# Gate and up with x's high and low parts side by side, and matmuls on few rows padded to 128

## Chip, cores and metric
The kernel runs on one core of a Trainium2 chip. The metric is the device time of one execution in microseconds; of several runs the median counts.

## The reference
Two layers over x of 256 tokens and 1024 features, float32. Each layer is

```
x = LN(alpha*x + 0.5 * (silu(x@Wg) * (x@Wu)) @ Wd)      # feed-forward, D_FF = 2816
x = LN(alpha*x + mixer(x))                              # MLA attention | mLSTM | retention, gated
x = LN(alpha*x + 0.5 * (silu(x@Wg) * (x@Wu)) @ Wd)      # second feed-forward
```

The mixer projects x to latents, queries, keys, values and gates. The attention branch has 4 heads: `score = q_nope . k_nope (128 features) + q_rope . k_rope (64 rotated features)`, causal, with a softmax; k_rope is shared by the heads. The mLSTM branch has 4 heads with exponential gates, for which a row of values per head must be spread over all 128 partitions. All weights are float32 and are read once.

## The kernel before
**Arithmetic.** TensorE (PE) takes the large products as float32r. Each float32 weight and each x is split into a high part (what the cast to float32r keeps) and a low part (the rest), and a product is three matmuls: high x high, high x low, low x high. This is `tile3` (lines 1177 to 1181), once per 128 input rows, accumulated in PSUM over the 8 chunks of 128 features. Small products (scores, values, sums over partitions) use plain float32, which PE does in two passes; the trace shows such a matmul as x2.

**Weights.** SyncE loads them in units of 128 x 2048 elements (1 MB) into a ring of three slots `raw` (`load`, line 337). ScalarE (ACT) casts a unit to `whi` (`hi`, line 456), VectorE (DVE) writes the rest to `wlo` (`lo`, line 724), PE uses both. `hi` waits until PE has left the slot (`w_used`), the next load until `lo` has read it (`w_lo`).

**Feed-forward.** A step handles 256 of the 2816 hidden features: unit gate, unit up, unit down, 11 steps a network, in a hardware loop except for the first and last pieces. In gate and up (`two_chunks`, `features`) the stationary operand is a 128x128 tile of weights, the moving one 256 tokens of x; 2 column tiles x 8 chunks x 3 matmuls = 48 matmuls of 256 columns. Gate goes to PSUM bank 4, up to bank 5, both column tiles side by side in one bank. ACT takes silu of bank 4 (line 467), DVE multiplies it with bank 5 (line 737) into `hid`, then splits `hid` (lines 744, 746). Down (`tokens`, line 1235) is 24 matmuls of 512 columns, with `hid` stationary and the weights moving, into banks 0 to 3, where alpha*x was put first as transposes (`seed`, line 1199). The order on PE is gate of step f+1, up of f+1, down of f. So `hid` of a step is needed one gate and one up unit after its own, but in the last step only one down unit after up's end. Each engine's order is written out by hand: on DVE in a turn the gate weights' `lo`, the product, the up weights' `lo`, the split of `hid`, the down weights' `lo`; on ACT the `hi` of gate, silu, `hi` of up, `hi` of down. In the last step the product and the split of `hid` come before the `lo` of the last down unit.

**Layer norm.** After each sub-layer the rows are normalised and transposed back; x is split pair by pair of chunks (`split_x`, lines 767 and 769) and the first unit of the next sub-layer takes each pair as it comes.

**Mixer.** Its order is also written by hand. Projection units of 48 matmuls alternate with small pieces. `mla_scores(h)` (lines 1319, 1320) adds for each of two query blocks a matmul over 128 features and one over the 64 rotary features; q_rope holds two heads on top of each other, heads of even number on partitions 0 to 63, odd on 64 to 127. k_rope holds the same 64 rows twice. The heads' scores run in pairs (0,1) and (2,3). `spread(h)` (line 1371) multiplies a selecting matrix on 4 rows with `row_m` on 4 rows, 512 columns, to give head h's row on all partitions. It is called in two pairs too. `rotate` (lines 851 to 854) makes q_rope and the others on DVE.

Of the kernel before, what the change touches and what calls it, by code (L numbers as in the profile page):

```python
# [100 lines left out]
def build(nc, a):  # L101
# [17 lines left out]
    def sem(name):  # L119
        return ctx.enter_context(nc.semaphore(name))  # L120
# [10 lines left out]
    xhi, xlo = sb("xhi", [P, KC, SEQ], F32R), sb("xlo", [P, KC, SEQ], F32R)  # L131
# [23 lines left out]
    hlo_last = place("hlo_last", [P, 2 * SEQ], F32R, r_u2 + 10240)  # L155
    g_row = place("g_row", [P, D_MODEL], F32, r_u2 + 16384)
# [15 lines left out]
    row_m = place("row_m", [HEADS, 2 * SEQ], F32, r_rows + 3072)  # L172
# [10 lines left out]

    k_rope = place("k_rope", [P, SEQ], F32, r_b)
    q_nope = place("q_nope", [P, HEADS, SEQ], F32, r_b + 1024)
    q_rope = place("q_rope", [P, 2, SEQ], F32, r_b + 5120)
# [43 lines left out]
    par_ready = sem("par_ready")  # L230

    silu_done, prod_done, hid_hi, hid_lo = sem("silu_done"), sem("prod_done"), sem("hid_hi"), sem("hid_lo")
    rows_loaded = sem("rows_loaded")
# [179 lines left out]
    def _(pool):  # L413

        pool.wait_ge(w_loaded[RING - 1], 16)
# [34 lines left out]
    def _(act):  # L450
# [7 lines left out]
        def ffn(l, w):  # L458
# [4 lines left out]
            def silu_of(j, k, f):  # L463

                act.wait_ge(w_used, done_no(l, k, f))
                act.wait_ge(prod_done, step_no(l, w, j))
                act.activation(silu[:, :], ps[:, 4, :], ACT.Silu).then_inc(silu_done, 1)  # L467

            hi(l, base + 2)
            silu_of(0, base, 0)  # L470
            hi(l, base + 3)
            hi(l, base + 4)
            with act.Fori(0, NF - 2) as f:
                hi(l, base + 5, f)
                silu_of(f + 1, base + 2, f)
                hi(l, base + 6, f)
                hi(l, base + 7, f)
            silu_of(NF - 1, base + 2, NF - 2)
# [240 lines left out]
    def _(dve):  # L719
# [7 lines left out]
        def ffn(l, w):  # L727
# [4 lines left out]
            def product(j, k, f):  # L732

                dve.wait_ge(silu_done, step_no(l, w, j))
                dve.wait_ge(w_used, done_no(l, k, f))
                dve.wait_ge(hid_lo, step_no(l, w, j))
                dve.scalar_tensor_tensor(out=hid[:, :], in0=ps[:, 5, :], scalar=0.5 / ALPHA, in1=silu[:, :],  # L737
                                         op0=ALU.mult, op1=ALU.mult).then_inc(prod_done, 1)

# [10 lines left out]
            product(0, base + 1, 0)  # L750
# [3 lines left out]
            with dve.Fori(0, NF - 2) as f:  # L754
                lo(l, base + 5, f)
                product(f + 1, base + 3, f)
# [912 lines left out]
```

## Time and profile before

| | |
|---|---|
| median of 3 runs | 1429.93 us (1428.03 to 1430.86) |
| profiled execution | 1428.79 us, its span 1426.6 us |
| mean granted clock of PE | 0.988 |
| busy: PE / DVE / ACT / POOL | 1378.0 / 865.7 / 617.4 / 66.1 us |
| matmuls | 9848 |
| DMA | 234.22 MB, mean 164 GB/s |

The span runs from the first to the last instruction; the time of an execution is a little longer. Matmuls are pipelined: the length that a row gives for one is from its start to its modelled end, and the next starts before that end. What one costs PE is the distance from its start to the next one's. "PEld" is the load of the stationary operand, which overlaps matmuls. A form such as `64*128 64x256` is a stationary operand of 64 rows by 128 columns and a moving one of 64 rows by 256 columns. "x24" on a row merges that many instructions in sequence. A bracket at the end of a row is the idle time before it and what ended it.

### The profile page before, as it was taken

How to read it: one execution, taken by the hardware profiler on the slowest of the kernel's cores; microseconds unless marked ns; L12 is line 12 of the kernel's file. 1: busy time of each engine (PE TensorE's matmuls, PEld its weight loads, DVE VectorE, ACT ScalarE, POOL GpSimd, SP SyncE). 2: the span in 40 equal slices, each digit the busy share in tenths (PEclk: the TensorE clock that was granted, in tenths of full speed). 3: DMA queues.
4: the chain of work that ended last, by engine and by line, in shares of the span. 5: the costliest groups of instructions: out<-in, count | busy, mean ns of one | idle time of the engine just before them, and what ended most of it. 6: DMA issues, size and time to landing. Idle time of an engine off the chain costs nothing.

```text
span 1426.6 us, 23193 instructions
## 1 busy us (share of the span) xinstructions
PE 1378.0 (97%) x9848; PEld 1285.4 (90%) x9848; DVE 865.7 (61%) x884; ACT 617.4 (43%) x586; POOL 66.1 (5%) x58
## 2 busy tenths in 40 slices
PE   7999989999999999999999999899999999999997
PEld 7999979889899979999899999797988999899996
DVE  4554466688885655544555544675888756554555
ACT  4333344564354353333443333554744543533331
POOL 2960000000000000000000000000000000000000
PEclk9999999999999999999999999999999999999999
DMA  8655644533345446555445555445334555465551
GB/s 285 209 176 178 192 146 129 178 116 122 118 158 190 167 137 206 177 179 192 159 154 193 183 176 187 131 142 158 119 91 146 178 178 177 121 203 176 183 196 63
DMA packets 182313, 234.22 MB, mean 164 GB/s; under 512 B 5808, under 2 KB 161072, under 8 KB 182128
## 3 DMA queue, kind: packets, MB, share of 16 engines
q1 hardware_dynamic: 182016, 231.68, 50.7%
q0 software_dynamic: 240, 1.71, 0.4%
q8 instruction: 44, 0.72, 0.2%
q14 instruction: 13, 0.11, 0.0%
HBM read 232.33 MB, written 1.05 MB: 164 GB/s over the span
## 4 chain that ended last, share of the span: by engine, by line
PE 95%; DVE 3%; ACT 2%; DMA 0%; issue 0%; SPq 0%; DVEq 0%; ACTq 0%
PE ps L1179 23%; PE ps L1180 23%; PE ps L1181 23%; PE ps L1235 20%; PE ps L1199 1%; DVE wlo L724 1%; PE ps L1334 1%; PE ps L1320 1%; DVE z L828 1%; PE ps L1371 1%; PE ps L1319 1%; ACT whi L456 1%; PE ps L1352 0%; PE ps L1381 0%; PE ps L1376 0%; DMA z<-x 0%
## 5 line engine op out<-in xcount | busy, mean ns | idle before, releaser
L456 ACT ACTIVATE whi<-raw 128x2048 fp32r<-128x2048 f32 (+2 forms) x221 | 416.2, 1883 | 665.2 <-PE ps L1181 489.3
L724 DVE TENSOR_TENSOR wlo<-raw,whi 128x2048 fp32r<-128x2048 f32 (+2 forms) x221 | 497.5, 2252 | 310.7 <-ACT whi L456 310.6
L1179 PE MATMUL ps<-xhi,whi 128*128 128x256 f32 (+1 forms) x2304 | 660.2, 287 | 15.6 <-DVE xlo L769 10.4
L1180 PE MATMUL ps<-xlo,whi 128*128 128x256 f32 (+1 forms) x2304 | 655.4, 284 | 0.0
L1181 PE MATMUL ps<-xhi,wlo 128*128 128x256 f32 (+1 forms) x2304 | 655.0, 284 | 0.0
L1179 PEld LDWEIGHTS ps<-xhi,whi 128*128 128x128 f32 (+1 forms) x2304 | 441.5, 192 | 22.7 <-issue 14.1
L1180 PEld LDWEIGHTS ps<-xlo,whi 128*128 128x128 f32 (+1 forms) x2304 | 441.4, 192 | 3.0 <-issue 0.5
L1181 PEld LDWEIGHTS ps<-xhi,wlo 128*128 128x128 f32 (+1 forms) x2304 | 441.6, 192 | 1.0
L1235 PE MATMUL ps<-wlo,hhi 128*128 128x512 f32 x320 | 127.7, 399 | 0.0
L1235 PE MATMUL ps<-whi,hhi 128*128 128x512 f32 x320 | 126.1, 394 | 0.0
L1235 PE MATMUL ps<-whi,hlo 128*128 128x512 f32 x320 | 125.4, 392 | 0.0
L737 DVE SCALAR_TENSOR_TENSOR hid<-ps,silu 128x512 f32<-128x512 f32 x44 | 30.5, 692 | 117.7 <-PE ps L1181 91.2
L1235 PEld LDWEIGHTS ps<-whi,hlo 128*128 128x128 f32 x320 | 60.1, 188 | 14.4
L1235 PEld LDWEIGHTS ps<-whi,hhi 128*128 128x128 f32 x320 | 60.2, 188 | 13.7
L1235 PEld LDWEIGHTS ps<-wlo,hhi 128*128 128x128 f32 x320 | 60.1, 188 | 12.1
L1179 PE MATMUL ps<-yhi,whi 128*128 128x256 f32 x192 | 54.6, 284 | 0.0
L1181 PE MATMUL ps<-yhi,wlo 128*128 128x256 f32 x192 | 53.7, 280 | 0.0
L1180 PE MATMUL ps<-ylo,whi 128*128 128x256 f32 x192 | 53.7, 280 | 0.0
L744 DVE CAST hhi<-hid 128x512 fp32r<-128x512 f32 x40 | 17.5, 438 | 48.4 <-PE ps L1235 48.4
L1179 PE MATMUL ps<-whi,xhi 128*128 128x256 f32 x128 | 38.2, 298 | 5.4 <-ACT k_nope L522 5.4
L467 ACT ACTIVATE silu<-ps 128x512 f32<-128x512 f32 x44 | 25.7, 584 | 32.9 <-PE ps L1181 32.9
L1180 PE MATMUL ps<-wlo,xhi 128*128 128x256 f32 x128 | 37.4, 292 | 0.0
(209 smaller groups left out, 1287.1 us busy)
## 6 DMA issues: line engine op xcount, KB each, us to landing
raw<-w_in SPq DMA_DIRECT2D x60, 1024.0 KB, 5.3
raw<-ffn_w_up SPq DMA_DIRECT2D x44, 1024.0 KB, 5.4
raw<-ffn_w_down SPq DMA_DIRECT2D x44, 1024.0 KB, 4.9
raw<-ffn_w_gate SPq DMA_DIRECT2D x43, 1024.0 KB, 5.3
raw<-w_br SPq DMA_DIRECT2D x12, 1024.0 KB, 5.1
raw<-w_out SPq DMA_DIRECT2D x8, 1024.0 KB, 5.0
raw<-mla_w_uq SPq DMA_DIRECT2D x4, 576.0 KB, 3.9
raw<-mla_w_ukv SPq DMA_DIRECT2D x2, 1024.0 KB, 5.0
```

The costliest lines, as they stand in the source:

```text
L456: act.activation(whi[:, k % RING, 0:n], raw[:, k % RING, 0:n], ACT.Copy).then_inc(w_hi, 1)
L467: act.activation(silu[:, :], ps[:, 4, :], ACT.Silu).then_inc(silu_done, 1)
L724: dve.tensor_tensor(wlo[:, k % RING, 0:n], raw[:, k % RING, 0:n], whi[:, k % RING, 0:n].bitcast(F32), ALU.subtract).then_inc(w_lo, 1)
L737: dve.scalar_tensor_tensor(out=hid[:, :], in0=ps[:, 5, :], scalar=0.5 / ALPHA, in1=silu[:, :], op0=ALU.mult, op1=ALU.mult).then_inc(prod_d ...
L744: dve.tensor_copy(dst_hi[:, :], hid[:, :]).then_inc(hid_hi, 1)
L828: dve.tensor_scalar(z[:, 1, part], ps[:, 2 + c, :], mv[:, 1, 0:1], rstd[:, 1:2], ALU.subtract, ALU.mult).then_inc(ln_rows1, 1)
L1179: pe.matmul(out, w_hi_ap, x_hi_ap, start=start, stop=False)
L1180: pe.matmul(out, w_hi_ap, x_lo_ap, start=False, stop=False)
L1181: return pe.matmul(out, w_lo_ap, x_hi_ap, start=False, stop=stop)
L1199: last = pe.matmul(ps[:, 2 * t + k // 4, (k % 4) * P:(k % 4 + 1) * P], xf[:, k, t * P:(t + 1) * P], ident, is_transpose=True, start=k % 4 ...
L1235: last = pe.matmul(ps[:, bank, :], x, w[:, kk, cols], start=start and i == 0, stop=stop and i == 2, skip_group_check=True)
L1319: pe.matmul(out[:, lo_c:hi_c], q_nope[:, h, tok], k_nope[:, h, 0:n], start=True, stop=False)
```

## The change
Gate and up get their own function `paired`. x's high and low parts lie side by side in one tensor `xpair`, chunk by chunk; `xhi` and `xlo` are views of it. For each tile one matmul of 512 columns takes the weight's high part with both parts of x, and one of 256 columns the weight's low part with x's high part, added to the first half. Each column tile has a bank of its own: gate banks 4 and 5, up banks 6 and 7. The second half of each bank (high x low) is copied to SBUF by ACT (`gsum`, `usum`) and added to the first half by DVE; silu and the product then read the sums. PE waits for the sums of the step before where it waited for silu and product. In the scores q_rope gets a plane per head with zeros in the rows that the head doesn't use, and the matmul takes 128 rows. The spread takes 128 rows too: `row_m` is now the top 4 rows of `rows_all`, which GpSimd clears at the start, and the selecting matrix is zero below row 4.

```diff
@@ -128,7 +128,8 @@
     whi, wlo = sb("whi", [P, RING, UNIT], F32R), sb("wlo", [P, RING, UNIT], F32R)
-    xhi, xlo = sb("xhi", [P, KC, SEQ], F32R), sb("xlo", [P, KC, SEQ], F32R)
+    xpair = sb("xpair", [P, KC, 2, SEQ], F32R)
+    xhi, xlo = xpair[:, :, 0, :], xpair[:, :, 1, :]
     xf = sb("xf", [P, KC, SEQ])
@@ -153,6 +154,8 @@
     hlo_last = place("hlo_last", [P, 2 * SEQ], F32R, r_u2 + 10240)
+    gsum = place("gsum", [P, 2 * SEQ], F32, r_u2 + 12288)
+    usum = place("usum", [P, 2 * SEQ], F32, r_u2 + 14336)
     g_row = place("g_row", [P, D_MODEL], F32, r_u2 + 16384)
@@ -169,7 +172,8 @@
     row_t = place("row_t", [HEADS, SEQ], F32, r_rows + 2048)
-    row_m = place("row_m", [HEADS, 2 * SEQ], F32, r_rows + 3072)
+    rows_all = place("rows_all", [P, 2 * SEQ], F32, r_rows + 3072)
+    row_m = rows_all[0:HEADS, :]
@@ -181,9 +185,9 @@
+    q_rope = place("q_rope", [P, HEADS, SEQ], F32, r_y + 20480)
     k_rope = place("k_rope", [P, SEQ], F32, r_b)
     q_nope = place("q_nope", [P, HEADS, SEQ], F32, r_b + 1024)
-    q_rope = place("q_rope", [P, 2, SEQ], F32, r_b + 5120)
     k_nope = place("k_nope", [P, HEADS, SEQ], F32, r_b + 7168)
@@ -228,8 +232,10 @@
     par_ready = sem("par_ready")
+    zeros_ready = sem("zeros_ready")
...
     silu_done, prod_done, hid_hi, hid_lo = sem("silu_done"), sem("prod_done"), sem("hid_hi"), sem("hid_lo")
+    gate_part, up_part, gate_summed, up_summed = sem("gate_part"), sem("up_part"), sem("gate_summed"), sem("up_summed")
     rows_loaded = sem("rows_loaded")
@@ -412,6 +418,7 @@
+        pool.memset(rows_all[:, :], 0.0).then_inc(zeros_ready, 1)
         pool.wait_ge(w_loaded[RING - 1], 16)
@@ -460,22 +467,39 @@
-            def silu_of(j, k, f):
+            def gate_of(j, k, f):
...
                 act.wait_ge(w_used, done_no(l, k, f))
+                act.wait_ge(silu_done, step_no(l, w, j) - 1)
+                act.activation(halves(gsum[:, :]), ps[:, 4:6, SEQ:], ACT.Copy).then_inc(gate_part, 1)
+            def silu_of(j):
+                act.wait_ge(gate_summed, step_no(l, w, j))
                 act.wait_ge(prod_done, step_no(l, w, j))
-                act.activation(silu[:, :], ps[:, 4, :], ACT.Silu).then_inc(silu_done, 1)
+                act.activation(silu[:, :], gsum[:, :], ACT.Silu).then_inc(silu_done, 1)
+            def up_of(j, k, f):
+                act.wait_ge(w_used, done_no(l, k, f))
+                act.activation(halves(usum[:, :]), ps[:, 6:8, SEQ:], ACT.Copy).then_inc(up_part, 1)
...
             hi(l, base + 2)
-            silu_of(0, base, 0)
+            gate_of(0, base, 0)
             hi(l, base + 3)
+            silu_of(0)
+            up_of(0, base + 1, 0)
             hi(l, base + 4)
             with act.Fori(0, NF - 2) as f:
+                gate_of(f + 1, base + 2, f)
                 hi(l, base + 5, f)
-                silu_of(f + 1, base + 2, f)
+                silu_of(f + 1)
+                up_of(f + 1, base + 3, f)
                 hi(l, base + 6, f)
                 hi(l, base + 7, f)
-            silu_of(NF - 1, base + 2, NF - 2)
+            gate_of(NF - 1, base + 2, NF - 2)
+            silu_of(NF - 1)
+            up_of(NF - 1, base + 3, NF - 2)
             hi(l, base + 3 * NF - 1)
@@ -729,13 +753,22 @@
-            def product(j, k, f):
+            def product(j):
+                dve.wait_ge(up_part, step_no(l, w, j))
+                dve.tensor_tensor(halves(usum[:, :]), ps[:, 6:8, 0:SEQ], halves(usum[:, :]), ALU.add)\
+                   .then_inc(up_summed, 1)
                 dve.wait_ge(silu_done, step_no(l, w, j))
-                dve.wait_ge(w_used, done_no(l, k, f))
                 dve.wait_ge(hid_lo, step_no(l, w, j))
-                dve.scalar_tensor_tensor(out=hid[:, :], in0=ps[:, 5, :], scalar=0.5 / ALPHA, in1=silu[:, :],
+                dve.wait_ge(up_summed, step_no(l, w, j))
+                dve.scalar_tensor_tensor(out=hid[:, :], in0=usum[:, :], scalar=0.5 / ALPHA, in1=silu[:, :],
                                          op0=ALU.mult, op1=ALU.mult).then_inc(prod_done, 1)
+            def gate_sum(j):
+                dve.wait_ge(gate_part, step_no(l, w, j))
+                dve.tensor_tensor(halves(gsum[:, :]), ps[:, 4:6, 0:SEQ], halves(gsum[:, :]), ALU.add)\
+                   .then_inc(gate_summed, 1)
@@ -747,17 +780,20 @@
             lo(l, base + 2)
-            product(0, base + 1, 0)
+            gate_sum(0)
+            product(0)
             lo(l, base + 3)
...
             with dve.Fori(0, NF - 2) as f:
+                gate_sum(f + 1)
                 lo(l, base + 5, f)
-                product(f + 1, base + 3, f)
+                product(f + 1)
                 lo(l, base + 6, f)
...
                 lo(l, base + 7, f)
-            product(NF - 1, base + 3, NF - 2)
+            gate_sum(NF - 1)
+            product(NF - 1)
             split(NF - 1, None, hhi_last, hlo_last)
@@ -851,7 +887,13 @@
                 dve.wait_ge(rot_parts, l * 6 + (r + 1))
-                dve.tensor_tensor(dst, wide(rot), wide(rot_sw), ALU.add).then_inc(rotated, 1)
+                if dst is None:
+                    for i in range(2):
+                        r_h = slice(ROPE * i, ROPE * i + ROPE)
+                        last = dve.tensor_tensor(q_rope[r_h, i::2, :], wide(rot)[r_h], wide(rot_sw)[r_h], ALU.add)
+                    last.then_inc(rotated, 1)
+                else:
+                    dve.tensor_tensor(dst, wide(rot), wide(rot_sw), ALU.add).then_inc(rotated, 1)
@@ -980,6 +1022,8 @@
             dve.memset(conv_in[:, :, 0:CONV - 1], 0.0).then_inc(conv_pad, 1)
+            for i in range(2):
+                dve.memset(q_rope[ROPE * i:ROPE * i + ROPE, 1 - i::2, :], 0.0)
             lo(l, m0 + 3)
@@ -1011,7 +1055,7 @@
             lo(l, m0 + 11)
-            rotate(1, q_rope[:, :, :], cos_m, sin_m)
+            rotate(1, None, cos_m, sin_m)
             lo(l, m0 + 12)
@@ -1205,11 +1249,6 @@
                 if stage is not None and kk % 2 == 0:
-                    if stage % 3 != 1:
-                        seed_ready(stage, kk // 2)
-                        seed(kk // 2)
-                    if stage == 0 and kk == KC // 2:
-                        pe.wait_ge(w_lo, done_no(0, 0))
                     pe.wait_ge(x_ready, stage * 4 + (kk // 2 + 1))
@@ -1225,6 +1264,26 @@
                                 None if c else stage)
+            return last
+        def paired(bank, k, stage=None):
+            wh, wl = slot(k, FB)
+            for c in range(2):
+                cols = slice(c * P, (c + 1) * P)
+                for kk in range(KC):
+                    if stage is not None and c == 0 and kk % 2 == 0:
+                        seed_ready(stage, kk // 2)
+                        seed(kk // 2)
+                        if stage == 0 and kk == KC // 2:
+                            pe.wait_ge(w_lo, done_no(0, 0))
+                        pe.wait_ge(x_ready, stage * 4 + (kk // 2 + 1))
+                    if kk:
+                        pe.matmul(ps[:, bank + c, 0:SEQ], wl[:, kk, cols], xhi[:, kk, :], start=False, stop=False)
+                    last = pe.matmul(ps[:, bank + c, :], wh[:, kk, cols], xpair[:, kk, :, :],
+                                     start=kk == 0, stop=kk == KC - 1)
+                    if kk == 0:
+                        pe.matmul(ps[:, bank + c, 0:SEQ], wl[:, kk, cols], xhi[:, kk, :], start=False, stop=False)
             return last
@@ -1241,14 +1300,14 @@
                 pe.wait_ge(w_lo, done_no(l, k, f))
-                pe.wait_ge(silu_done, step_no(l, w, j) - 1)
-                two_chunks(4, k).then_inc(w_used, 1)
+                pe.wait_ge(gate_summed, step_no(l, w, j) - 1)
+                paired(4, k).then_inc(w_used, 1)
...
                 if j is not None:
-                    pe.wait_ge(prod_done, step_no(l, w, j))
-                two_chunks(5, k).then_inc(w_used, 1)
+                    pe.wait_ge(up_summed, step_no(l, w, j) - 1)
+                paired(6, k).then_inc(w_used, 1)
@@ -1268,7 +1327,7 @@
                 pe.wait_ge(w_lo, done_no(l, base))
-            two_chunks(4, base, stage=l * 3 + 2 * w).then_inc(w_used, 1)
+            paired(4, base, stage=l * 3 + 2 * w).then_inc(w_used, 1)
             up_of(None, base + 1, 0)
@@ -1312,12 +1371,11 @@
-                r = slice(64 * (h % 2), 64 * (h % 2) + 64)
                 out = ps[:, BANK[f"S{h}"], :]
...
                     pe.matmul(out[:, lo_c:hi_c], q_nope[:, h, tok], k_nope[:, h, 0:n], start=True, stop=False)
-                    last = pe.matmul(out[:, lo_c:hi_c], q_rope[r, h // 2, tok], k_rope[r, 0:n], start=False, stop=True)
+                    last = pe.matmul(out[:, lo_c:hi_c], q_rope[:, h, tok], k_rope[:, 0:n], start=False, stop=True)
                 last.then_inc(s_done, 1)
@@ -1368,7 +1426,8 @@
-                pe.matmul(ps[:, BANK[f"bc{h}"], :], C("sel", P, h * P)[0:HEADS, :], row_m[:, :],
+                pe.wait_ge(zeros_ready, 1)
+                pe.matmul(ps[:, BANK[f"bc{h}"], :], C("sel", P, h * P), rows_all[:, :],
                           start=True, stop=True).then_inc(bc_done, 1)
```

## Rows read from the trace of the kernel before

**Rows 1.** The page's chain that ended last, by engine.
```profile
PE 95%; DVE 3%; ACT 2%; DMA 0%; issue 0%; SPq 0%; DVEq 0%; ACTq 0%
```

**Rows 2.** The chain in order of time (start us, length us, what), both layers.
```profile
544.67 5.60 PE ps L1235 x24
561.77 5.60 PE ps L1235 x24
```

**Rows 3.** Stretches: length, busy PE PEld DVE ACT POOL, PEclk, DMA, GB/s.
```profile
561.77:578.87 17.10, 17.10 (x121) 16.00 (x121) 8.69 (x6) 6.23 (x4) 0.00 (x0) 1.00 0.56 184
```

**Rows 4.** Timeline of PE (start, length): first 64-wide matmul, first after them.
```profile
227.28 0.28 PE L1179 MATMUL ps<-xhi,whi 128*64 128x256 f32 x1
...
230.00 0.28 PE L1179 MATMUL ps<-xhi,whi 128*128 128x256 f32 x1
```

**Rows 5.** Timeline of PE inside a down unit.
```profile
109.38 0.39 PE L1235 MATMUL ps<-whi,hhi 128*128 128x512 f32 x1
109.61 0.40 PE L1235 MATMUL ps<-wlo,hhi 128*128 128x512 f32 x1
109.85 0.39 PE L1235 MATMUL ps<-whi,hlo 128*128 128x512 f32 x1
```

**Rows 6.** Groups of instructions; the last row with shapes kept apart.
```profile
L456 ACT ACTIVATE whi<-raw 128x2048 fp32r<-128x2048 f32 (+2 forms) x221 | 416.2, 1883 | 665.2 <-PE ps L1181 489.3
...
L737 DVE SCALAR_TENSOR_TENSOR hid<-ps,silu 128x512 f32<-128x512 f32 x44 | 30.5, 692 | 117.7 <-PE ps L1181 91.2
...
L467 ACT ACTIVATE silu<-ps 128x512 f32<-128x512 f32 x44 | 25.7, 584 | 32.9 <-PE ps L1181 32.9
...
L767 DVE CAST xhi<-xf 128x512 fp32r<-128x512 f32 x24 | 10.1, 420 | 9.5 <-ACT xf L698 9.5
```

**Rows 7.** Timeline of DVE in the last step of a network.
```profile
698.66 0.69 DVE L737 SCALAR_TENSOR_TENSOR hid<-ps,silu 128x512 f32<-128x512 f32 x1 [7.32 <-PE ps L1181]
...
700.46 4.49 DVE L724 TENSOR_TENSOR wlo<-raw,whi 128x2048 fp32r<-128x2048 f32 x2
```

**Rows 8.** Timeline of PE, where the last down unit begins.
```profile
704.01 0.39 PE L1235 MATMUL ps<-whi,hhi_last 128*128 128x512 f32 x1
```

**Rows 9.** Timeline of PE: scores of two heads, and the unit after.
```profile
287.63 0.39 PE L1319 MATMUL ps<-k_nope,q_nope 128*128 128x128 f32 x2
...
291.71 0.39 PE L1179 MATMUL ps<-xhi,whi 128*128 128x256 f32 x1
291.93 0.28 PE L1180 MATMUL ps<-xlo,whi 128*128 128x256 f32 x1
```

**Rows 10.** Timeline of PE: values of one head.
```profile
303.98 0.59 PE L1334 MATMUL ps<-pt,v_mla 128*128 128x256 f32 x2
...
304.63 0.60 PE L1334 MATMUL ps<-pt,v_mla 128*128 128x256 f32 x2
```

**Rows 11.** Timeline of PE: two row spreads, and the unit after.
```profile
316.50 1.98 PE L1371 MATMUL ps<-row_m,cst 4*128 4x512 f32 x4
318.40 0.39 PE L1179 MATMUL ps<-xhi,whi 128*128 128x256 f32 x1
318.63 0.28 PE L1180 MATMUL ps<-xlo,whi 128*128 128x256 f32 x1
```

**Rows 12.** Timeline of PE: a mean on 128 rows, and what follows.
```profile
343.10 1.02 PE L1376 MATMUL ps<-ht,cst 128*128 128x512 f32 x2
343.96 0.38 PE L1352 MATMUL ps<-ml_qk 128*128 128x256 f32 x1
```

**Rows 13.** Waits in 379 to 400 us: who waited for whom, us, times, longest.
```profile
PE ps L1179 <- ACT rg L522: 2.6, 1, 2.6
```

**Rows 14.** Timeline of DVE near the start of the first mixer.
```profile
220.85 2.29 DVE L724 TENSOR_TENSOR wlo<-raw,whi 128x2048 fp32r<-128x2048 f32 x1 [4.78 <-ACT whi L456]
```

**Rows 15.** The stretches view, two places after layer norms.
```profile
716.70:720.10 3.40, 3.40 (x19) 3.40 (x17) 3.33 (x6) 2.84 (x2) 0.00 (x0) 0.50 0.71 289
513.00:524.00 11.00, 7.64 (x58) 6.25 (x57) 9.95 (x18) 8.58 (x13) 0.00 (x0) 1.00 0.27 95
```

## The prediction, made before the changed kernel ran
> **What bounds the kernel now.** I read the chain of waits first: TensorE (PE) holds 95% of the span [rows 1]. In order of time the chain repeats every 17.10 us inside a feed-forward network; 5.60 us of each turn is one down unit of 24 matmuls (line 1235), the rest gate and up (lines 1179 to 1181) [rows 2]. The stretches say the same: in one turn PE is busy 17.10 of 17.10 us, VectorE (DVE) 8.69, ScalarE (ACT) 6.23, at full clock, with the DMA engines at 0.56 [rows 3]. So a step is worth its PE time, and work added to DVE or ACT is free while it stays off PE's waits.
>
> **Gate and up.** Of the 17.10 us gate and up are 11.50: 96 matmuls of 256 columns, 0.1198 us each. The down unit gives 5.60/24 = 0.2333 us for one of 512 [rows 2]. Per tile the change puts one matmul of 512 and one of 256 in the place of three of 256: 0.3531 us against 0.3594, 6.25 ns less. A unit has 16 tiles and there are 88 gate and up units (2 layers, 2 networks, 22 each): 1408 x 6.25 ns = 8.8 us less. PE streams as many columns as before; one weight load in three goes, with what it costs the stream.
> No row shows this mixture, so I bound it. The 24 matmuls of 256 columns whose weights are 64 wide start at 227.28, the unit after them at 230.00: 0.1133 us each [rows 4]. That is the stream with nearly no cost of loading; twice it, 0.2267, is the best case for the wide matmul: 12.9 ns less per tile, 18.2 us. Within the down unit the starts are 0.23 and 0.24 apart, by which operands meet [rows 5]; 0.24 each would give no gain (+0.6 us). I take the mean, 0.2333: the same form (128-wide weights, 512 columns), and it lies as far above 2 x 0.1133 (6.6 ns) as one load costs the 256-column matmul (6.5 ns).
> The Trainium skill's page TensorE: Matmul & The Clock Gate, section Back-to-back issue gap, gives 262 cycles for 256 columns and 518 for 512 at full clock. Three of the first against one of each saves 6 cycles, by my estimate 2.5 ns a tile or 3.5 us in all. The trace does not agree: 0.1198 us is 10% above its 262 cycles.
>
> **What the wider form adds.** The products with x's high and low parts now stand in two halves of a bank and must be added. Per step ACT gets two copies of 128x512 from PSUM (as the silu, 0.58 us) and DVE two additions (as the product, 0.69) [rows 6]: ACT 6.23 + 1.2 = 7.4, DVE 8.69 + 1.4 = 10.1 of 16.9 us, beside PE.
> The waits: gate's copy stands ahead of a cast on ACT (1.9 us [rows 6]), up's copy ahead of the next, and the product ahead of up's weight split on DVE (2.25 [rows 7]). In the loop, counted from the end of up: copy to 0.6, sum to 1.3, product to 2.0; cast to 2.6, split of the next up weights to 4.9, which PE needs at 5.6 + 5.65 = 11.2; hid is split after down at 5.6, as before. Gate's weights are ready 4.8 us after gate's end, needed at 11.2. The sums on which PE itself waits are those of the step before. No stall.
> In the last step of each network the cover is thin. DVE took the product at 698.66 and began the last two weight splits at 700.46, the first of them (the last down unit's) to 702.7; PE began that unit at 704.01 [rows 7, 8]: 1.3 us to spare. Now copy and sum (0.6 + 0.75) come first and the split ends about 704.1. PE waits 0.1 to 0.2 us, four times: 0.7 us. The cast of those weights, now behind up's copy on ACT, ends 2.6 us after up, before DVE reaches the split at 3.2. Bounds 0 to 2 us.
> Splitting x now writes rows that stand 512 columns apart. Such a cast takes 0.42 us; an operation of that size at the slower rate 0.69 [rows 6]. If the new pattern cost that, each of six stages would start about 0.8 us later, 5 us in all; the inner run stays 256 contiguous elements, so I take nothing.
>
> **Scores.** There are four groups of two heads. Each takes 287.63 to 291.71 = 4.08 us, matmuls on 64 and on 128 rows alternating [rows 9]. The values, whose matmuls are all on 128 rows, take 303.98 to 304.63 = 0.65 us for one of 256 columns and one of 128, in the same two-pass form [rows 10]. A pair of heads has four of each: 2.60 us. So 1.48 less, four times: 5.9. The first matmul after the 64-row ones takes 0.22 us (291.71 to 291.93) where others take 0.12, in two of the groups: 6.1 us together. Bounds 0 (the gaps are not from the rows) to 6.3.
> **Row spread.** Two spreads take 316.50 to 318.40 = 1.90 us, four passes of 512 columns on 4 rows, and 0.23 for the first matmul after [rows 11]. A mean, on 128 rows, takes two such passes in 343.10 to 343.96 = 0.86 us [rows 12]. 0.18 + 0.11 = 0.29, four times: 1.2 us. Bounds 0 to 2.
> Is that on the path? After the scores PE stands for long only once a layer, 2.6 us for ACT's copy of rg [rows 13], which begins from the end of a PE unit and so shifts with PE; DVE's softmax chain starts from the scores and shifts with them. Two memsets of q_rope per layer fall in DVE's idle 4.78 us at 220.85 [rows 14]; the addition that is now two (0.69 more) has until the scores at 287.63. GpSimd's memset of the rows is its first instruction, long before the spread. SP's queue is untouched; its loads follow the weight splits, at most 1.4 us later, with the DMA engines half idle. All nothing.
> The Trainium skill's same page says in its closing table that one matmul on 32 rows takes the time of one on 128. That speaks against this part: filling rows would buy nothing, which is rival C. The 4-row passes (0.475) and the 128-row ones (0.43) do not bear it out.
>
> **Sum.** -8.8 - 6.1 - 1.2 + 0.7 = -15.4 us. The profiled execution took 1428.8 us, 2.2 outside its span: 1413.4. The median of the runs stands 1.1 above it: 1414.5.
>
> **The clock** is noise on both sides. After the idle gap of a layer norm PE may be granted half clock (1.2 of 2.4 GHz) for a stretch, as at 716.70; the gap at 513 us, like it, had none [rows 15]. Such a stretch costs up to 1.7 us. With shifted times one or two may come or go: 3 us either way.
>
> **Rivals.**
> A, the wide matmul pays per column, 0.24 us. For it: one start in [rows 5]; against: the others. 1429.9 + 0.6 - 7.3 + 0.7 = 1423.9. Chance 0.14.
> B, the load is wholly hidden behind 512 columns, 0.2267. For it: [rows 4]; against: the down unit's mean. 1429.9 - 18.2 - 7.3 + 0.7 = 1405.1. Chance 0.12.
> C, padding buys nothing; the gaps come from the operands. Against: [rows 10, 12]. 1429.9 - 8.8 + 0.7 = 1421.8. Chance 0.06.
> D, slower: the 256-column matmul adds to half of the bank that the 512-column one has just written, and must let it drain. That one lasts 0.39 us and its successor starts after 0.233 [rows 5], so a full drain is 0.16 us x 1408 = 225 us: about 1648. It decides from 15.4 us / 1408 = 11 ns a tile. Against: in [rows 10] the 128-column matmul adds to half of what the 256-column one wrote, without a gap. Chance 0.05.
> The forecast has 0.60; 0.03 is left for small new waits. A difference of 0.2% (2.9 us) is what a measurement here can tell from none. Faster 0.91, same 0.04, slower 0.05. The range takes in A and C, and of B all but its end: 1406 to 1424.
>
> **What would show it.** A turn of 16.90 us (5.60 + 32 x 0.3531) with PE busy throughout; wide matmuls followed after 0.233 us, narrow ones after 0.120; pairs of heads in 2.6 us; two spreads in 1.72; a wait of 0.1 to 0.2 us ahead of the last down unit. Wrong would be a turn of 17.1 or more, PE idle in the loop with line 724 as releaser, or x's splits slower than 0.42 and 0.69 us.

## The result, and the profile after

The changed kernel took 1404.18 us (median of 4 runs, 1402.68 to 1408.41) against 1428.98 us for the kernel before on the same chip (4 runs, 1424.81 to 1430.86). The ratio is 0.9837, 95% interval 0.981 to 0.9864: faster by 24.8 us, where 15.4 us less and 1414.5 had been forecast. The time lies 1.8 us below the low end of the range. The direction and each mechanism held; the size of the largest term did not, and the clock gave between 5 and 6 us that no term held.

The profiled execution took 1403.12 us with a span of 1400.8 (before: 1426.6). The page's chain that ended last (answers to [rows 1]):

```profile
PE 95%; DVE 3%; ACT 2%; issue 0%; DMA 0%; SPq 0%; DVEq 0%; ACTq 0%
```

The same chain in order of time, start, length, what (answers to [rows 2]; line 1294 is the down unit's matmul):

```profile
553.57 5.59 PE ps L1294 x24
...
570.36 5.59 PE ps L1294 x24
```

And the stretch from one down unit to the next (answers to [rows 3]; length, then busy time of PE, PEld, DVE, ACT, POOL, then PEclk, DMA share, GB/s):

```profile
553.57:570.36 16.79, 16.79 (x90) 14.26 (x89) 10.07 (x8) 7.24 (x6) 0.00 (x0) 1.00 0.58 187
```

The reader is to see three things. PE still holds the chain. A turn is 16.79 us in place of 17.10, all of it gate and up: 16.79 - 5.59 = 11.20 for 32 tiles, 0.3500 us a tile, where 0.3531 was forecast and 0.3594 stood before. And DVE (10.07) and ACT (7.24) took the new additions and copies, at the sizes forecast (10.1 and 7.4), beside a PE that is busy for the whole turn. The groups of the page show the two forms and the new work (busy, mean ns of one, then idle before and its releaser):

```profile
L1283 PE MATMUL ps<-xpair,whi 128*128 128x512 f32 x1408 | 489.5, 397 | 5.0 <-DVE xpair L805 5.0
L1282 PE MATMUL ps<-xpair,wlo 128*128 128x256 f32 x1232 | 345.5, 280 | 0.0
...
L474 ACT ACTIVATE gsum<-ps 128x512 f32<-128x512 f32 x44 | 26.4, 599 | 167.1 <-PE ps L1283 167.1
L759 DVE TENSOR_TENSOR usum<-ps,usum 128x512 f32<-128x512 f32 x44 | 30.4, 691 | 89.9 <-ACT usum L485 89.9
L770 DVE TENSOR_TENSOR gsum<-ps,gsum 128x512 f32<-128x512 f32 x44 | 30.4, 691 | 85.3 <-ACT gsum L474 85.3
```

A matmul's length in these rows (397, 280 ns) is not its price, since the next starts long before it ends. The price is the distance between starts, in PE's timeline:

```profile
559.47 0.40 PE L1283 MATMUL ps<-xpair,whi 128*128 128x512 f32 x1
559.70 0.28 PE L1282 MATMUL ps<-xpair,wlo 128*128 128x256 f32 x1
559.82 0.39 PE L1283 MATMUL ps<-xpair,whi 128*128 128x512 f32 x1
560.05 0.27 PE L1282 MATMUL ps<-xpair,wlo 128*128 128x256 f32 x1
560.16 0.40 PE L1283 MATMUL ps<-xpair,whi 128*128 128x512 f32 x1
```

Two tiles take 559.47 to 560.16 = 0.69 us. Over the 1408 tiles, without the few matmuls at half clock or ahead of a wait, the wide one is followed after 233.9 ns on average and the narrow one after 115.8 (112 to 120).

The scores of two heads (answers to [rows 9]), then two row spreads with what follows (answers to [rows 11]):

```profile
284.04 0.39 PE L1377 MATMUL ps<-k_nope,q_nope 128*128 128x128 f32 x2
284.26 0.39 PE L1378 MATMUL ps<-k_rope,q_rope 128*128 128x128 f32 x2
284.48 0.60 PE L1377 MATMUL ps<-k_nope,q_nope 128*128 128x256 f32 x2
284.92 0.59 PE L1378 MATMUL ps<-k_rope,q_rope 128*128 128x256 f32 x2
...
286.78 0.28 PE L1224 MATMUL ps<-xpair,whi 128*128 128x256 f32 x1
```

```profile
309.89 1.88 PE L1430 MATMUL ps<-rows_all,cst 128*128 128x512 f32 x4
311.21 0.68 PE L1223 MATMUL ps<-xpair,whi 128*128 128x256 f32 x1
311.73 0.28 PE L1224 MATMUL ps<-xpair,whi 128*128 128x256 f32 x1
```

The first matmul behind such a group starts early and is followed late, so I go to the second. From the first score to the second matmul after them: 2.74 us, before 4.30 (287.63 to 291.93). The second group of a layer, with other work behind it, goes from 4.21 to 2.85. From the first spread to the second matmul after it: 1.84 us, before 2.13, at all four places.

Last, the end of a network (answers to [rows 7, 8]). DVE, then PE:

```profile
689.36 0.69 DVE L764 SCALAR_TENSOR_TENSOR hid<-usum,silu 128x512 f32<-128x512 f32 x1
690.08 0.43 DVE L777 CAST hhi_last<-hid 128x512 fp32r<-128x512 f32 x1
690.54 0.69 DVE L779 TENSOR_TENSOR hlo_last<-hid,hhi_last 128x512 fp32r<-128x512 f32 x1
691.15 4.49 DVE L748 TENSOR_TENSOR wlo<-raw,whi 128x2048 fp32r<-128x2048 f32 x2
```

```profile
693.07 0.40 PE L1294 MATMUL ps<-whi,hlo 128*128 128x512 f32 x1
693.49 0.50 PE L1294 MATMUL ps<-whi,hhi_last 128*128 128x512 f32 x1
693.83 0.40 PE L1294 MATMUL ps<-wlo,hhi_last 128*128 128x512 f32 x1
```

693.07 to 693.83 is 0.76 us where two matmuls take 0.47: PE loses 0.29 us. The four ends are alike (0.29 to 0.30 lost at each) and cost 1.2 us; 0.7 had been forecast.

**Work and clock apart.** The granted clock differs between kernels and between runs of one kernel: 0.983 to 0.993 in 40 later runs of the kernel before, 0.988 to 0.992 in four after. Where PE holds the chain, lost clock is lost time, so I also give each span multiplied by its mean granted clock, as a measure of the work: 1408.3 us before (mean of those 40 runs), 1389.2 after, 19.1 less. The measure is rough. It takes a lost clock as wholly lost time, and over those 40 runs that is a little too much: the product is 1408.2 as a mean of the 17 runs at 0.986 and 1409.7 for the 3 at 0.993. The clock is also read to 0.001, which is 1.4 us of span. By stage, in the two profiled executions, from one layer norm's last statistics to the next's and with half of each half clock stretch taken off: the second and third feed-forward networks 196.1 to 192.9 and 195.9 to 192.8 us, the two mixers 305.4 to 301.8 and 305.0 to 301.8. The rest of the 24.8, 5.7 us, is clock: (1 - 0.988) x 1426.6 = 17.1 us before, (1 - 0.992) x 1400.8 = 11.2 after.

### The profile page after: what moved, and what is told of

Same layout as the page of the kernel before. It is cut to its first block, busy times and chain, and to the rows that moved or that the text cites. A ratio compares the mean times of both kernels' runs of the same rounds, so it can differ in the third digit from the quotient of the medians.

```text
span 1400.8 us, 20707 instructions
## 1 busy us (share of the span) xinstructions
PE 1353.8 (97%) x8440; PEld 1203.2 (86%) x8440; DVE 928.8 (66%) x978; ACT 663.4 (47%) x674; POOL 69.9 (5%) x59
## 4 chain that ended last, share of the span: by engine, by line
PE 95%; DVE 3%; ACT 2%; issue 0%; DMA 0%; SPq 0%; DVEq 0%; ACTq 0%
PE ps L1283 24%; PE ps L1294 21%; PE ps L1223 11%; PE ps L1224 11%; PE ps L1225 11%; PE ps L1282 10%; PE ps L1286 1%; DVE wlo L748 1%; PE ps L1243 1%; PE ps L1392 1%; DVE z L864 1%; ACT whi L463 1%; PE ps L1410 0%; PE ps L1430 0%; PE ps L1440 0%; PE ps L1435 0%
## 5 line engine op out<-in xcount | busy, mean ns | idle before, releaser
L1283 PE MATMUL ps<-xpair,whi 128*128 128x512 f32 x1408 | 489.5, 397 | 5.0 <-DVE xpair L805 5.0
L1282 PE MATMUL ps<-xpair,wlo 128*128 128x256 f32 x1232 | 345.5, 280 | 0.0
L1283 PEld LDWEIGHTS ps<-xpair,whi 128*128 128x128 f32 x1408 | 255.2, 188 | 54.5 <-DVE xpair L805 5.7
L1223 PE MATMUL ps<-xpair,whi 128*128 128x256 f32 (+2 forms) x896 | 259.7, 290 | 10.7 <-DVE xpair L805 5.4
L1224 PE MATMUL ps<-xpair,whi 128*128 128x256 f32 (+2 forms) x896 | 255.9, 286 | 0.0
L1225 PE MATMUL ps<-xpair,wlo 128*128 128x256 f32 (+2 forms) x896 | 255.8, 286 | 0.0
L1282 PEld LDWEIGHTS ps<-xpair,wlo 128*128 128x128 f32 x1232 | 233.1, 189 | 8.1
L1223 PEld LDWEIGHTS ps<-xpair,whi 128*128 128x128 f32 (+2 forms) x896 | 170.4, 190 | 13.4 <-issue 12.4
L1224 PEld LDWEIGHTS ps<-xpair,whi 128*128 128x128 f32 (+2 forms) x896 | 170.3, 190 | 2.0 <-issue 1.0
L1225 PEld LDWEIGHTS ps<-xpair,wlo 128*128 128x128 f32 (+2 forms) x896 | 170.3, 190 | 1.0
L759 DVE TENSOR_TENSOR usum<-ps,usum 128x512 f32<-128x512 f32 x44 | 30.4, 691 | 89.9 <-ACT usum L485 89.9
L770 DVE TENSOR_TENSOR gsum<-ps,gsum 128x512 f32<-128x512 f32 x44 | 30.4, 691 | 85.3 <-ACT gsum L474 85.3
```

Of the source, the lines that this page charges most:

```text
L759: dve.tensor_tensor(halves(usum[:, :]), ps[:, 6:8, 0:SEQ], halves(usum[:, :]), ALU.add)\
L770: dve.tensor_tensor(halves(gsum[:, :]), ps[:, 4:6, 0:SEQ], halves(gsum[:, :]), ALU.add)\
L1223: pe.matmul(out, w_hi_ap, x_hi_ap, start=start, stop=False)
L1224: pe.matmul(out, w_hi_ap, x_lo_ap, start=False, stop=False)
L1225: return pe.matmul(out, w_lo_ap, x_hi_ap, start=False, stop=stop)
L1282: pe.matmul(ps[:, bank + c, 0:SEQ], wl[:, kk, cols], xhi[:, kk, :], start=False, stop=False)
```

## The experiments

Each is a change to the kernel before or to the changed one, timed beside the kernel before, in three sessions (e1 to e4, e5 to e8, e9 to e11), in which the kernel before had medians of 1428.42, 1428.71 and 1428.0 us over 11, 14 and 15 runs. The last column is span times clock, the mean over the runs.

| kernel | median, us | ratio to before, 95% | clock, median | span x clock |
|---|---|---|---|---|
| before, by session | 1428.42, 1428.71, 1428.0 | | 0.987, 0.987, 0.988 | 1408.6, 1408.0, 1408.4 |
| changed | 1404.18 | 0.9837 (0.981 to 0.9864) | 0.991 | 1389.2 |
| e1 pairing alone | 1411.57 | 0.9893 (0.9859 to 0.9927) | 0.991 | 1396.6 |
| e2 paddings alone | 1418.88 | 0.9938 (0.9919 to 0.9956) | 0.988 | 1400.4 |
| e3 pair unfused | 1416.96 | 0.9926 (0.9899 to 0.9953) | 0.992 | 1403.0 |
| e4 grouped | 1405.68 | 0.9844 (0.981 to 0.9879) | 0.990 | 1388.6 |
| e5 last step | 1406.30 | 0.9848 (0.9819 to 0.9877) | 0.988 | 1386.8 |
| e6 strict order | 1402.48 | 0.9822 (0.9793 to 0.9852) | 0.993 | 1389.9 |
| e7 scores alone | 1419.14 | 0.9928 (0.9902 to 0.9953) | 0.990 | 1403.4 |
| e8 before, shifted | 1432.58 | 1.0026 (1.0008 to 1.0045) | 0.986 | 1411.0 |
| e9 strict, last step | 1402.60 | 0.9826 (0.981 to 0.9843) | 0.992 | 1388.8 |
| e10 changed, shifted | 1407.52 | 0.9849 (0.983 to 0.9869) | 0.990 | 1391.3 |
| e11 spread alone | 1424.18 | 0.9976 (0.9962 to 0.999) | 0.991 | 1408.2 |

(One run of e6 has a span of 1400.3 us beside a clock of 0.944, which its span does not show; it is left out of that row's product.)

**The parts by themselves.** e1 is the changed kernel with the scores and the spread as before (the two lines on which it rests; the layout of q_rope, its memsets and its addition go back too):

```
-  pe.matmul(..., q_rope[:, h, tok], k_rope[:, 0:n], start=False, ...)
+  pe.matmul(..., q_rope[r, h // 2, tok], k_rope[r, 0:n], start=False, ...)
-  pe.matmul(..., C("sel", P, h * P), rows_all[:, :], ...)
+  pe.matmul(..., C("sel", P, h * P)[0:HEADS, :], row_m[:, :], ...)
```

> Gate and up paired as in the changed kernel; scores and row spread as before. Theory H (hidden load): a 256-column matmul beside 512-column ones has its own weights loaded early and costs 0.116 us in place of 0.120, so a turn of the loop stays 16.79 us as in the changed kernel, and the whole gains 1408 x 9.4 ns = 13.2 less about 1.2 for the waits before the last down units: 12.0 us, some 1417. My forecast's sizing (0.2333 + 0.1198 us a tile) would give turns of 16.90 and some 1421. Theory K (clock): 3 to 4 us of the measured gain are half-clock stretches that happened not to occur, so this and the run with padding alone add up to about 19 us, not 25.

e2 is the kernel before with these edits the other way round, that is, with both paddings and without the pairing.

> Scores and row spread on 128 rows, gate and up as before. All theories: two heads' scores in 2.63 us in place of 4.08, two spreads in 1.72 in place of 1.90; turns of 17.10 us. Gain 7.3 us, some 1421.7, with 3 us either way from half-clock stretches. If padding bought nothing, as rival C had it, the time would be that of before.

Measured: 12.0 us less work with pairing alone, 8.2 with the paddings alone, 20.2 together against 19.1 for the whole change. Within what the measure can tell the parts add up; I see no sign that one feeds on the other. In e1 the turn is 16.79 us and a mixer takes 305.4 us as before; in e2 the second network takes 196.1 us as before, and the mixers 301.1 and 301.3. In time, the two gains are 16.9 and 9.5 us: each is larger than its work, by what its clock gave.

e7 does only the scores, e11 only the spread.

> The kernel before with only the rotary scores on 128 rows padded with zeros; gate and up and the row spread as before. Theory: each pair of heads goes from 4.08 us to 2.63, and a layer's four pairs give 5.8 to 6.1 us in the whole; with the clock as before 1422.6 at the median. The rest of what both paddings gave together (9.5 us at the median, 8.2 when each span is multiplied by its granted clock) is then the row spread's and the clock's. Rival: the spread gives more than its 16 matmuls show (0.7 us a layer), because the work behind it starts sooner, and then the scores alone give under 5, 1424 or more.

> The kernel before with only the row spread on 128 rows. Theory: 16 matmuls per layer that take 0.43 us in place of 0.475, 0.7 us a layer at most 1.4 in the whole: near 1427.5 with the clock of before. Rival: what both paddings gave beyond the scores (3.0 us in the profiles at full clock: 1398.6 to 1395.6) is all the spread's: 1425.5.

By the rows the two parts come out clean. In e7 and in e2 every group of scores takes what it takes in the changed kernel, in e11 and in e2 every pair of spreads, and what was not edited takes what it took before. With half of the half clock time taken off, e7's mixers take 302.1 us each, 3.3 and 2.9 less: 6.2 for the scores (6.1 forecast; the rows give 2 x (1.56 + 1.36) = 5.8). e11's take 304.7, 0.7 and 0.3 less: 1.0 for the spread (1.2 forecast; the rows give 4 x 0.29 = 1.2). The stage figure of e11 alone would not carry that, since the same sum for e8's mixers, which nobody touched, is 0.3 and for the first mixer of e10 0.9. (e11's expectation counts 16 matmuls a layer; the trace has 8 passes, so its 0.7 us is for both layers.) Both forecasts stand, and the rival of e11 falls. Span times clock does less well at this size: it gives 4.6 us for e7 and 0.2 for e11, 4.8 together, where e2 had 8.2 and the rows give 7.0.

Now look at the medians: e11 gained 3.8 us and e7 9.6, with about 1 and 6 us of work taken out. So a kernel with hardly less work was 0.24% faster, with an interval (0.9962 to 0.999) that does not reach 1.

**What the wide matmul is worth.** e3 keeps x's parts side by side, the copies and the additions, but runs the wide one as two of 256 columns:

```
-  last = pe.matmul(ps[:, bank + c, :], wh[:, kk, cols], xpair[:, kk, :, :], start=kk == 0, ...)
+  pe.matmul(ps[:, bank + c, 0:SEQ], wh[:, kk, cols], xhi[:, kk, :], start=kk == 0, stop=False)
+  last = pe.matmul(ps[:, bank + c, SEQ:], wh[:, kk, cols], xlo[:, kk, :], start=False, ...)
```

> The changed kernel, but the 512-column matmul is split again into two of 256 columns with the same weights loaded twice; banks, copies, sums and the layout of x stay. Theory H: all matmuls of gate and up are narrow again and cost 0.120 us: turns of 17.10 us, 13.2 us over the changed kernel, some 1417. Theory L (layout): the narrow matmul became cheaper by where x and the banks lie, not by its neighbours: turns of about 16.8 us (5.60 + 96 x 0.117) and some 1405.

Its down units start 17.10 us apart:

```profile
541.02 5.60 PE ps L1296 x24
...
558.12 5.60 PE ps L1296 x24
```

All of the turn's gain is gone, and the starts are 0.120 us apart again. So neither the layout nor the two halves of the bank pay anything; the form of 512 columns does, together with its narrow neighbour. Note its clock too: 0.991 or 0.992 in five runs of five, with no matmul of 512 columns in gate and up.

e4 runs the eight wide ones of a column tile first, then the eight narrow ones (the narrow ones inside the first loop are taken out):

```
   for kk in range(KC):
       pe.matmul(ps[:, bank + c, :], wh[:, kk, cols], xpair[:, kk, :, :], start=kk == 0, stop=False)
+  for kk in range(KC):
+      last = pe.matmul(ps[:, bank + c, 0:SEQ], wl[:, kk, cols], xhi[:, kk, :], start=False, ...)
```

> The changed kernel with another order: per column tile first the 8 wide matmuls, then the 8 narrow ones. Theory H: 7 of 8 narrow matmuls follow a narrow one and so have their load beside 256 columns only: 0.120 us; a turn is 16.79 + 28 x 0.004 = 16.90 us and the whole 5 us over the changed kernel, some 1409. Theory L: the order doesn't matter, 16.79 us and no change.

Its chain, which shows the two forms apart:

```profile
557.66 5.60 PE ps L1293 x24
563.26 1.85 PE ps L1281 x8
565.11 0.95 PE ps L1284 x8
566.07 1.84 PE ps L1281 x8
567.91 0.95 PE ps L1284 x8
568.86 1.84 PE ps L1281 x8
```

Eight narrow ones take 0.95 us, 0.119 each, as the theory of the hidden load had it; but eight wide ones take 1.845, 0.2306 each (0.2304 over all of them), not the 0.234 of the changed kernel. A tile takes (1.845 + 0.95) / 8 = 0.349 us, as in the changed kernel. e6, strictly wide, narrow, wide, narrow, is a third order:

```
   pe.matmul(ps[:, bank + c, :], wh[:, kk, cols], xpair[:, kk, :, :], start=kk == 0, stop=False)
   last = pe.matmul(ps[:, bank + c, 0:SEQ], wl[:, kk, cols], xhi[:, kk, :], start=False, ...)
```

> The changed kernel, with each wide matmul followed by the narrow one of the same contraction tile: strictly wide, narrow, wide, narrow, where the change has two narrow ones in a row once and two wide ones in a row once per column tile. Theory H (a narrow matmul streams in 116 ns when the weight load behind it is done under a wide one; beside another narrow one it takes 119 to 120, and a wide one beside a wide one takes 231): the two effects cancel, the turn of the loop stays within 0.05 us of 16.79 and the time within 2 us of 1404.2. Rival O (the pair of neighbours narrow, narrow is what keeps the narrow mean at 116.0 and not lower, and strict order brings it to 113 with the wide at 233): 3 ns per narrow, 0.1 us per turn, 4 us off, near 1400.

It gives 233.3 ns behind a wide one and 117.1 behind a narrow one: 350.4. In three orders the tile comes out at 349 to 350 ns while the shares move by 3 ns between the two forms. The theory that a narrow one is cheap because the next load hides beside a wide one had the narrow one's share right, but not the wide one's, and falls as a price: its 16.90 us turn for e4 was 16.78. With the 231 ns that e4 showed put in for a wide one behind a wide one, as e6's expectation does, it fits all three orders; that figure was read from e4 and not predicted. e6's rival falls.

**The wait at the end of a network.** e5 makes the last down unit's parts earlier:

```
 # ScalarE
   silu_of(NF - 1)
+  hi(l, base + 3 * NF - 1)
   up_of(NF - 1, base + 3, NF - 2)
-  hi(l, base + 3 * NF - 1)
 # VectorE
   gate_sum(NF - 1)
+  lo(l, base + 3 * NF - 1)
   product(NF - 1)
   split(NF - 1, None, hhi_last, hlo_last)
-  lo(l, base + 3 * NF - 1)
```

> The changed kernel, with the high and low parts of the last down unit's weights made ahead of the last up unit's copy and product in each of the four feed-forward stages. In the profile of the changed kernel that unit takes 5.88 us where the others take 5.59, with TensorE waiting 0.29 us in it behind VectorE's product, hidden parts and weight low part. Theory W (that order makes the wait): the unit takes 5.59, four times 0.29 = 1.2 us off the span, near 1403.0 at the median. Rival V (the weight's low part ahead of the product makes the hidden parts late, and the unit starts late): the unit takes 5.59 but TensorE waits ahead of it, no gain or up to 1 us lost, 1404.2 to 1405.2.

PE at the same place in e5:

```profile
691.50 0.40 PE L1294 MATMUL ps<-whi,hlo 128*128 128x512 f32 x1
691.74 0.39 PE L1294 MATMUL ps<-whi,hhi_last 128*128 128x512 f32 x1
691.97 0.39 PE L1294 MATMUL ps<-wlo,hhi_last 128*128 128x512 f32 x1
```

The wait is gone: 0.47 us for what took 0.76. In the profiles the second and third networks go from 192.9 and 192.8 us to 192.6 and 192.5. Span times clock falls by 2.4, of which four waits explain 1.2. The rest is not shown to be the edit's: the first network, whose start also depends on when x lands, has 1.3 of it in the profile, and e9 against e6, the same edit once more, has 1.1 in all. The time did not follow: 1406.30, because all four runs had a clock of 0.987 or 0.988. e9 has e5's edit and e6's order together.

> The changed kernel with both edits: strictly wide, narrow in each tile, and the last down unit's parts made ahead of the last up unit's copy and product. Theory: the two hardly touch each other; with half of the half clock time taken off each span, strict order left the changed kernel's 1389 as it was and the earlier parts took 2.4 us from it, so 1387 here, and a median of 1400.0 to 1401.5 at a granted clock of 0.991 (1399.5 to 1404 over the clocks seen). Rival: the early parts bring the clock of the run that had them (0.988 in four runs of four), and the time is 1403 to 1406 in spite of the work saved.

e9 took 1402.60 us, with the waits gone and a clock of 0.992: 1.6 us below the changed kernel's median, less than 0.2%, which a measurement here cannot tell from nothing. It was 1.1 us over the upper end of what I expected of it, though inside the wider one.

**The clock.** e8 and e10 put eight more copies of the first transposes ahead of everything, in the kernel before and in the changed one:

```
   seed_ready(stage, kk // 2)
+  if stage == 0 and kk == 0:
+      for _ in range(8):
+          seed(0)
   seed(kk // 2)
```

> The kernel before, with eight more copies of its first transposes of x at the very start, some 3.5 us of TensorE work that changes no result and shifts all that follows against the clock's own windows. Each span multiplied by its granted clock has been 1408.6 as a mean over 11 runs of the kernel before, at granted clocks from 0.986 to 0.993. Theory P (which seams fall to half clock is a matter of where they fall in time, so the clock's part of a difference is no property of the change): span times clock rises by the 3 to 4 us added, and the granted clock takes another value in the range 0.985 to 0.993, with time anywhere from 1423 to 1434. Rival S (the clock is a property of the instruction stream: the separate narrow streams of gate and up lose it, the paired ones keep it): the granted clock stays at 0.986 to 0.988 as a median, the half clock stretch of 6.8 us behind the second layer's mixer, at 972.7 us in the profile of before, appears again 3 to 4 us later, and the time is 1432.

> The changed kernel with eight more copies of its first transposes of x at the very start, which in the kernel before added 2.3 us and left its granted clock at 0.986. Theory S (which seams run at half clock goes with the stream of work, not with where it falls in time): the same 2.3 us, clock 0.988 to 0.992 as without, time 1406.5. Theory P (a matter of timing): the clock leaves that range, or its stretches turn up at other seams, as the second layer's seam behind the mixer near 959 us, and the time is 1408 to 1412.

They added 3.0 and 2.1 us by span times clock. e8 kept the clock of before (0.986 in 6 of 10 runs) and the same places at half clock, each some 2 us later, as its rival S had said; but S, by which separate narrow streams lose the clock, falls by e3. e10 was at 0.990 in three of four, within theory S's range, with a new place at half clock at 269.9 us, as theory P allowed; its 1407.52 us lies between the two. The place where before and after differ most is behind the second layer's first projections. The stretches view there, of before, of the changed kernel and of e5:

```profile
972.70:979.50 6.80, 6.18 (x29) 6.19 (x30) 2.77 (x6) 0.71 (x3) 0.00 (x0) 0.50 0.95 298
```

```profile
957.00:964.00 7.00, 4.38 (x36) 4.38 (x37) 5.55 (x8) 2.70 (x5) 0.00 (x0) 1.00 0.87 273
```

```profile
957.00:963.80 6.80, 6.15 (x29) 6.15 (x30) 3.58 (x7) 0.74 (x3) 0.00 (x0) 0.50 0.94 298
```

Before, PE ran 6.8 us at 1.2 GHz there, at a cost of up to 3.4. The changed kernel has none. Yet PE had stood idle for the same time ahead of both, 2.7 us up to 973.32 and up to 959.62, for ACT's copy of k_nope. The waits view has it with its twin in the first layer (us in total, times, longest; before, then changed):

```profile
PE ps L1179 <- ACT k_nope L522: 5.4, 2, 2.7
```

```profile
PE ps L1223 <- ACT k_nope L546: 5.4, 2, 2.7
```

e5, which also pairs gate and up, has the place at half clock again, and e3, which does not pair them, has the better clock. So the better clock is no property of the pairing. Nor is it of a mere shift, by e8, though that was one shift of one size. What decides it stays open. The kernel before alone, with the same instructions each time, ran at anything from 0.983 to 0.993.

## Why the prediction was right or wrong

**Bound.** Right. PE holds 95% of the chain before and after, and a turn has no idle PE.

**Gate and up, 8.8 us forecast.** This is the step that failed, in its size: the price of a tile in the mixture, 0.3531 us forecast and 0.3500 measured. Measured: 0.3594 - 0.3500 = 9.4 ns x 1408 = 13.2 us. The prediction priced the wide one at the down unit's mean, 0.2333 us; measured 0.2339, 0.2333 and 0.2304 in three orders (changed, e6, e4). It priced the narrow one at 0.1198, what it costs in a row of its own kind; measured 0.1158, 0.1171 and 0.1190. In the changed kernel it is thus the narrow one that cost 4 ns less than its price.

Why the tile comes to 350 ns is not shown. Two other sums give it after the fact. By the down unit's rate per column, 5.60 us / 24 = 0.2333 us per 512 columns, a tile of 768 columns takes 0.2333 x 1.5 = 0.350 us; that would have given 13.2 us and a forecast of 1410.1. The other takes the wide price from the closer of the down unit's starts. In the trace of before these are 0.2315, 0.2378 and 0.2305 us apart on average, by which operands meet, and e4's wide ones, in a stream of their own, took 0.2304: with 0.231 + 0.1198 = 0.351 the gain would have been 12 us. The runs have one mixture only and cannot tell the two apart.

The trace of before also held a row against 0.1198. The same form over y and over the latent rows is cheaper. Of line 1179 in the kernel before, weight loads and matmuls of three streams (min/median/max ns):

```profile
L1179 PEld LDWEIGHTS ps<-xhi,whi x2304: 84/192/337, 13.6 to 1404.9; 128*128 128x128 f32 x188, 128*64 128x64 f32 x2, 128*4 128x4 f32 x2
L1179 PE MATMUL ps<-xhi,whi x2304: 276/283/682, 13.7 to 1405.0; 128*128 128x256 f32 x188, 128*64 128x256 f32 x2, 128*4 128x256 f32 x2
L1179 PEld LDWEIGHTS ps<-yhi,whi x192: 187/188/194, 397.5 to 1194.4; 128*128 128x128 f32 x192
L1179 PE MATMUL ps<-yhi,whi x192: 277/280/682, 397.5 to 1194.5; 128*128 128x256 f32 x192
```

Loads of 188 ns in place of 192 and matmuls of 280 in place of 283, and their starts are 117.6 ns apart on average, not 120. The forecast's best case (rival B, 0.2267 + 0.1198 = 0.3465) was not reached either. That 1404.18 us lies next to B's 1405.1 is chance: the tile took 3.5 ns more than B's, and the clock made up for it.

**New work on DVE and ACT, forecast hidden.** Right: 0.60 and 0.69 us a piece beside PE. x's splits kept their 0.42 and 0.69 us in the wider layout, as taken.

**The wait in the last step, +0.7.** Right in place and cause (e5 takes it away), too small in size: 0.29 us four times, 1.2. PE was due at 693.30 and started at 693.49, 0.19 us late, at the upper end of the 0.1 to 0.2; and that first matmul took a further 0.1 us to be followed, which the forecast did not have.

**Scores, -6.1, and spread, -1.2.** Right: 1.56 us for the first and 1.36 for the second group of a layer, 5.8 in all against 6.1 forecast; 0.29 per two spreads against 0.29. Rival C (padding buys nothing) falls by e2. The padding changes two things at once, how many rows a matmul has and, for the heads of odd number, on which partition they begin; no run tells these apart. The closing table of the Trainium skill's page TensorE: Matmul & The Clock Gate says that one matmul on 32 rows takes the time of one on 128. The traces here do not agree for matmuls on 64 rows amid others on 128 (4.30 against 2.74 us a group), nor for those on 4 rows (2.13 against 1.84 us for two spreads).

**Clock, 3 us either way.** Too narrow. Work gave, by the rows, 13.2 + 7.0 - 1.2 = 19.0 us, where span times clock has 19.1, and the medians 24.8. A place at half clock that came or went was allowed for at up to 1.7 us, one or two of them; in fact a gain of 3.4 at one place and of 1.7 at another (1225.3 us) were there in one direction. Spans of the kernel before alone ran from 1419.6 to 1430.4 us.

Rivals A and D fall by the timeline: the wide one costs 0.234, not 0.240, and the narrow one starts 0.23 us after it with no drain.

## What to carry to other kernels

Treat the price of a new mixture of matmuls as a range. The trace of before offered three sums for one tile: 0.3531 us from the means of two streams, 0.351 with the closer of the down unit's starts, 0.350 by that unit's rate per column. They are 1% apart, and yet the first took a third off the gain, since a gain is a small difference of large prices. Which of them holds in another mixture, no run here shows. Where fp32 matmuls on few rows stand among matmuls on 128, compare the gap with a full-row pair in the same trace: here zero rows cost PE nothing and gave back a third of the time of a group of scores. And before a difference under half a per cent is explained by the work, look at the granted clock of each run: an edit worth 1 us of work measured 3.8. For edits that small the rows of the trace are the measure; span times clock was out by 1 to 2 us.

## What the runs showed of the hardware that had not been expected

- A stream of 256 columns with 128-wide weights from x starts every 120 ns exactly once it has run for about ten matmuls (before: 117 to 121 at first, then 120 throughout; loads of 192 ns), while the same form over y or the latent rows stays at 115 to 123, mean 117.6. In e3 x's stream is at 120 with x in another layout. Why x's stream differs was not found.
- Wide and narrow matmuls trade 3 ns between them by their order, 233.9 and 115.8 ns, 233.3 and 117.1, 230.4 and 119.0, and the sum stays within 349.4 to 350.4.
- Half clock stretches come and go with edits of 1 to 2 us of work, and from run to run of one kernel. The cause was not settled.
